# Seven block products in the second half of three output projections and of two down products

## What the reference computes

```python
x = x + (silu(gate) * sparse_attention(rms_norm(x))) @ a_w_out          # layer a
x = x + (silu(gate) * block_attention(rms_norm(x))) @ b_w_out           # layer b
proj = rms_norm_2(x) @ w_in                                             # layer c
q, k, v = split(silu(causal_conv_4(proj[dn_qkv])))                      # gated deltanet branch
q, k = l2norm(q), l2norm(k)                                             # sums of squares over a head
mixed = g_nsa * (o_nsa @ w_up_nsa) + g_dn * (o_dn @ w_up_dn)
x = x + mixed @ w_o
h2 = rms_norm_2(x)                                                      # layer d
x = x + (silu(h2 @ w_gate) * (h2 @ w_up)) @ w_down                      # 5632 hidden columns
return rms_norm_2(x)
```

## Time and profile before

| | |
|---|---|
| median of 3 runs | 2228.33 us (2227.85 to 2229.3) |
| profiled execution, its own time | 2230.15 us |
| its span, first to last instruction | 2228.8 us |
| mean granted TensorE clock | 0.999 |
| PE busy | 2208.3 us, 11376 instructions |
| DVE busy | 1529.6 us, 2034 instructions |
| ACT busy | 1216.5 us, 1682 instructions |
| POOL busy | 115.6 us |

### The profile page before, as it was taken

The page is one execution under the profiler, slowest core; times in us unless marked ns, Lnnn a source line. Parts: engine busy times, 40 slices in busy tenths (PEclk is TensorE's granted clock), DMA queues, the critical chain, the costliest instruction groups (busy, mean ns, idle before and its releaser), DMA issues.

```text
span 2228.8 us, 29092 instructions
## 1 busy us (share of the span) xinstructions
PE 2208.3 (99%) x11376; PEld 1825.2 (82%) x11376; DVE 1529.6 (69%) x2034; ACT 1216.5 (55%) x1682; POOL 115.6 (5%) x101
## 2 busy tenths in 40 slices
PE   9999999999999999999999999999999999999998
PEld 7888888888888887888888888888888888888886
DVE  5687765767765677675755556768887578855885
ACT  5545665645665664464544546556555355543554
POOL 0002210003220121000000000000000000000000
PEclk9999999999999999999999999999999999999999
DMA  7456677655677675444644446776666665665674
GB/s 257 143 176 177 196 195 232 202 189 173 201 212 233 195 209 143 142 133 147 223 161 151 151 151 196 231 213 190 210 234 200 203 197 187 214 229 177 202 243 150
DMA packets 313386, 427.31 MB, mean 192 GB/s; under 512 B 121057, under 2 KB 121217, under 8 KB 313121
## 3 DMA queue, kind: packets, MB, share of 16 engines
q1 hardware_dynamic: 311088, 418.35, 59.3%
q0 software_dynamic: 1584, 6.16, 1.0%
q10 hardware_dynamic: 576, 0.95, 0.1%
HBM read 396.06 MB, written 2.10 MB: 179 GB/s over the span
## 4 chain that ended last, share of the span: by engine, by line
PE 92%; issue 3%; DVE 2%; ACT 1%; DMA 1%; POOL 1%; SPq 0%; DVEq 0%; ACTq 0%; POOLq 0%
PE ACC L1127 19%; PE ACC L1129 19%; PE ACC L1128 19%; PE ACC L988 3%; PE ACC L989 3%; PE ACC L990 3%; PE SCPV L988 3%; PE SCPV L989 3%; PE SCPV L990 3%; PE SCPV L1060 1%; PE ACC L1059 1%; PE SCPV L1058 1%; PE SCPV L1059 1%; PE ACC L1060 1%; PE ACC L1058 1%
## 5 line engine op out<-in xcount | busy, mean ns | idle before, releaser
L2257 DVE TENSOR_TENSOR WL<-W,WH 128x1024 fp32r<-128x1024 f32 x729 | 894.0, 1234 | 399.3 <-ACT WH L1156 165.8
L1156 ACT ACTIVATE WH<-W 128x1024 fp32r<-128x1024 f32 x729 | 744.8, 1049 | 248.7 <-PE ACC L1129 93.6
L1127 PE MATMUL ACC<-WH,XH 128*128 128x512 f32 x1888 | 764.9, 405 | 4.0 <-ACT arena L1156 3.0
L1129 PE MATMUL ACC<-WH,XL 128*128 128x512 f32 x1888 | 737.1, 390 | 0.0
L1128 PE MATMUL ACC<-WL,XH 128*128 128x512 f32 x1888 | 735.4, 389 | 0.0
L1127 PEld LDWEIGHTS ACC<-WH,XH 128*128 128x128 f32 x1888 | 354.8, 188 | 80.9 <-issue 6.0
L1129 PEld LDWEIGHTS ACC<-WH,XL 128*128 128x128 f32 x1888 | 354.3, 188 | 76.5
L1128 PEld LDWEIGHTS ACC<-WL,XH 128*128 128x128 f32 x1888 | 355.2, 188 | 68.9 <-issue 1.2
L1156 ACT ACTIVATE arena<-arena 128x1024 uint16<-128x1024 uint16 (+5 forms) x98 | 87.1, 893 | 68.9 <-DVE arena L1948 26.0
L1156 ACT ACTIVATE arena<-ACC,reciprocal_roots 128x512 f32<-128x512 f32 x86 | 58.6, 687 | 118.5 <-PE ACC L1129 118.0
L988 PE MATMUL ACC<-WH,XH 128*128 128x512 f32 x264 | 103.2, 391 | 0.0
(11 more groups left out here) (378 smaller groups left out, 2657.5 us busy)
## 6 DMA issues: line engine op xcount, KB each, us to landing
W<-in_w_in SPq DMA_DIRECT2D x84, 1024.0 KB, 5.0
W<-in_a_w_in SPq DMA_DIRECT2D x47, 1024.0 KB, 5.4
W<-in_w_ffn_gate SPq DMA_DIRECT2D x44, 1024.0 KB, 5.4
W<-in_w_ffn_up SPq DMA_DIRECT2D x44, 1024.0 KB, 5.2
W<-in_w_ffn_down SPq DMA_DIRECT2D x44, 1024.0 KB, 5.2
W<-in_b_w_in SPq DMA_DIRECT2D x40, 1024.0 KB, 5.2
W<-in_a_w_out SPq DMA_DIRECT2D x16, 1024.0 KB, 5.8
W<-in_b_w_out SPq DMA_DIRECT2D x16, 1024.0 KB, 6.2
```

The lines of the kernel that those rows point to most:

```text
L1127: MM(out, hx, WH[:, k, 0:ch.width], start=q == 0 and k == 0, stop=False)
L1129: ins = MM(out, lx, WH[:, k, 0:ch.width], start=False, stop=last and k == QK - 1)
L1156: return nc.scalar.activation(out, in_, func, **how)
L2257: TT(tiles_of(M.WL[K.pair(n)], ch, half), raw, tiles_of(M.WH[n % 3], ch, half).bitcast(F32), ALU.subtract).then_inc(*did("weights_rest", n ...
```

## The change

The double chunk and the block become general. `WITH_BLOCK` names five double chunks whose third slab in order (`order_of`: slabs 0, 2, 1, 3) is a block with seven products: a.o23, b.o23, c.o23, d.p0c23 and d.p1c23. Each output projection becomes two double chunks, o01 without a block and o23 with one. b.k and b.v become b.kv, c.q0 and c.k0 become c.qk0 (c.nar follows both). d.p2c2 and d.p2c3 stay single. The block's first part is at quads 4 and 5 of the chunk; two plain quads follow.

A new block does on DVE what a pair's does (four `combine`, three `combination_rest`) and, in place of the pair's joins, eight operations of 128x512 (`joins`); ACT copies product 1 and rounds three combinations. `forms` is made for each new set of tokens (five times more; for parts 1 and 2 of the pairs again as well, since the room is shared: eight times in all), seven quads ahead of a down or projection block. The side tasks move with the chunks: `x` is now complete for two column groups at a time.

The core of the diff; the seven products themselves are the function `pair` had them in, now `seven_products`, in the same order:

```diff
+TWO = {"b.kv": ("b.k", "b.v"), "c.qk0": ("c.q0", "c.k0")}
+WITH_BLOCK = ("a.o23", "b.o23", "c.o23", "d.p0c23", "d.p1c23")
...
+def order_of(ch):
+
+    return (0, 2, 1, 3) if ch.name in WITH_BLOCK else tuple(range(ch.quads // 2))
+
+
+def place_of(ch):
+
+    return 3 if ch.taker == "pair" else 2 if ch.name in WITH_BLOCK else None
...
+            add("b.kv", one(w, 2048), "two", quads=8, fresh=x)
...
-        for c in range(NC_D):
-            add(f"{l}.o{c}", one(o, c * CH), "dve", fresh="go." + l if c == 0 else None)
+        add(f"{l}.o01", one(o, 0), "both", quads=8, fresh="go." + l)
+        add(f"{l}.o23", one(o, 2 * CH), "both", quads=8)
...
+                add("c.qk0", one(w, DN_COL), "two", quads=8, fresh="x.c")
...
+        if p < len(FF_PARTS) - 1:
+            add(f"d.p{p}c23", one("w_ffn_down_2", 2 * CH), "both", quads=2 * n, row0=done * CH, xs="H")
...
     for before, l in (("a", "b"), ("b", "c"), ("c", "d")):
-        for c in range(NC_D):
-            begin(after(f"{before}.o{c}"), "squares", l, c)
-        for c in range(3):
-            begin(after(f"{before}.o{c}") + 1, "halves", "x." + l, c)
-            begin(first(before + ".o3") + 4 * (c + 1), "joined", "x." + l, c)
-        begin(after(before + ".o3"), "halves", "x." + l, 3)
-        begin(after(before + ".o3") + 1, "roots", l)
-        begin(after(before + ".o3") + 7, "joined", "x." + l, 3)
+        for n in (before + ".o01", before + ".o23"):
+            for c in range(2):
+                begin(after(n) - 4 + 5 * c, "squares", l, int(n[-2]) + c)
+                begin(after(n) - 4 + 8 * c, "halves", "x." + l, int(n[-2]) + c)
+        for c, visit in enumerate((first(before + ".o23") + 9, first(before + ".o23") + 25, after(before + ".o23") + 3, after(before + ".o23") + 11)):
+            begin(visit, "joined", "x." + l, c)
+        begin(after(before + ".o23") + 2, "roots", l)
...
-            begin(after(f"c.{n}0") + 9 + 4 * s, "dn_conv", 0, s, c)
+            begin(after(f"c.{n}0") + 9 + 6 * (n == "k") + 4 * s, "dn_conv", 0, s, c)
             begin(after("c.v1") + 5 + 4 * (2 * c + s), "dn_conv", 1, s, c)
     for s in range(2):
-        begin(after("c.k0") + 13 + 4 * s, "dn_norms", 0, s)
+        begin(after("c.k0") + 19 + 4 * s, "dn_norms", 0, s)
...
+    def joins(b, steps):
+
+        block, to = K.blocks[b], M.JOIN[K.blocks[b].tokens]
+        g, u, col = block.quad, block.quad + 1, block.chunk.parts[0][1]
+        x = lambda t, c: M.X[:, t, col + c * CH:col + (c + 1) * CH]
+        first, second = to[:, 0, :], to[:, 1, :]
+        for i in steps:
+            if i == 0:
+                dve.wait_ge(*at("product_copied", b))
+                ins = TT(x(0, 0), first, x(0, 0), ALU.add)
+            if i == 1:
+                dve.wait_ge(*at("multiplied", g, 0, 1))
+                dve.wait_ge(*at("join_step", b, 0))
+                ins = TT(first, TP[1][:, :], first, ALU.add)
+            if i == 2:
+                dve.wait_ge(*at("multiplied", u, 0, 1))
+                dve.wait_ge(*at("join_step", b, 1))
+                ins = TT(second, PV[1][:, :], first, ALU.add)
+            if i == 3:
+                dve.wait_ge(*at("join_step", b, 2))
+                ins = TT(x(0, 1), second, x(0, 1), ALU.add)
+            if i == 4:
+                ins = TT(x(1, 1), second, x(1, 1), ALU.add)
+            if i == 5:
+                dve.wait_ge(*at("multiplied", u, 1, 1))
+                ins = TT(first, TP[0][:, :], first, ALU.add)
+            if i == 6:
+                dve.wait_ge(*at("join_step", b, 4))
+                ins = TT(x(1, 1), TP[0][:, :], x(1, 1), ALU.add)
+            if i == 7:
+                dve.wait_ge(*at("join_step", b, 5))
+                ins = TT(x(1, 0), first, x(1, 0), ALU.add)
+            ins.then_inc(*did("join_step", b, i))
...
+        if where == (-1, 0, 0):
+            combine(b, 1)
+            combine(b, 2)
+        if where == (-1, 0, 1):
+            combine(b, 3)
+        if where == (0, 0, 0):
+            combine(b, 4)
+            combination_rest(b, 2)
+        if where == (0, 0, 1):
+            if j is not None:
+                gate_left(j)
+            combination_rest(b, 4)
+            combination_rest(b, 3)
+        if where == (0, 1, 0):
+            if j is not None:
+                joined_products(j)
+            else:
+                joins(b, (0, 1, 2))
+        if where == (1, 0, 0):
+            if j is not None:
+                up_left(j)
+            else:
+                joins(b, (3, 4))
+        if where == (1, 1, 0):
+            if j is not None:
+                last_product(j)
+            else:
+                joins(b, (5, 6))
+        if where == (2, 0, 0) and j is None:
+            joins(b, (7,))
...
+        first_of = {block.tokens: b for b, block in reversed(list(enumerate(K.blocks)))}
+        ahead = lambda block: 2 if block.tokens == "gate and up 0" else 4 if block.chunk.taker == "pair" else 7
+        K.forms_at = {K.blocks[b].quad - ahead(K.blocks[b]): b for b in first_of.values()}
```

More of the change, by code:

```diff
@@ L150, with block_plan @@
 Chunk = namedtuple("Chunk", "name first quads parts width row0 k0 xs fresh taker tiles")
+def order_of(ch):
+    return (0, 2, 1, 3) if ch.name in WITH_BLOCK else tuple(range(ch.quads // 2))
+def place_of(ch):
+    return 3 if ch.taker == "pair" else 2 if ch.name in WITH_BLOCK else None
+Block = namedtuple("Block", "quad chunk tokens source slice room")
+def block_plan(chunks):
+    blocks, part = [], 0
+    for ch in chunks:
+        if ch.taker != "pair" and ch.name not in WITH_BLOCK:
+            continue
+        if ch.taker == "pair":
+            part = sum(int(ch.name[4:]) >= start for start in FF_STARTS) - 1
+            tokens, source, room = f"gate and up {part}", "x.d", "d"
+        elif ch.xs == "H":
+            tokens, source, room = f"down {part}", f"h{part}.d", "d"
+        else:
+            tokens, source, room = ch.name[0], {"a": "go.a", "b": "go.b", "c": "mx.c"}[ch.name[0]], ch.name[0]
+        place = place_of(ch)
+        blocks.append(Block(ch.first + 2 * place, ch, tokens, source, order_of(ch)[place], room))
+    return blocks
 def weight_plan():
@@ L194, in weight_plan @@
         add(f"c.ud{c}", one("w_up_dn_2", c * CH), "dve", quads=2, k0=8, fresh="od.c" if c == 0 else None)
-    for c in range(NC_D):
-        add(f"c.o{c}", one("w_o_2", c * CH), "dve", fresh="mx.c" if c == 0 else None)
+    add("c.o01", one("w_o_2", 0), "both", quads=8, fresh="mx.c")
+    add("c.o23", one("w_o_2", 2 * CH), "both", quads=8)
     done = 0
@@ L996, in pair, with seven_products @@
+    def seven_products(ch, x, visit, ends):
+        b, hi, lo = K.block_at[ch.first + 2 * place_of(ch)], M.hi[ch.xs], M.lo[ch.xs]
+        block = K.blocks[b]
+        g, u = block.quad, block.quad + 1
+        tokens = lambda a, t, k: a[:, QK * x + k:QK * x + k + HK, t * P:(t + 1) * P]
         A11, A12, A22 = [(tokens(hi, t, k), tokens(lo, t, k)) for t, k in ((0, 0), (0, HK), (1, HK))]
-        S1, S2, S3, S4 = [(M.form_hi[:, i], M.form_lo[:, i]) for i in range(4)]
-        place = lambda n, half: (M.WH[n % 3][:, half * HK:(half + 1) * HK, :], M.WL[K.pair(n)][:, half * HK:(half + 1) * HK, :])
@@ L1000, in product @@
[L1000 removed]
+        form_hi, form_lo = M.FORMS[block.room]
+        S1, S2, S3, S4 = [(form_hi[:, i], form_lo[:, i]) for i in range(4)]
+        weights = lambda n, half: (M.WH[n % 3][:, half * HK:(half + 1) * HK, :], M.WL[K.pair(n)][:, half * HK:(half + 1) * HK, :])
+        def product(out, form, w, first, last):
             nonlocal visit
             for k in range(HK):
[L1003 to L1005 removed]
+                MM(out, form[0][:, k, :], w[0][:, k, :], start=first and k == 0, stop=False)
+                MM(out, form[0][:, k, :], w[1][:, k, :], start=False, stop=False)
+                ins = MM(out, form[1][:, k, :], w[0][:, k, :], start=False, stop=last and k == HK - 1)
@@ L1010, in pair @@
             for half in range(2):
-                pe.wait_ge(*at("turned", ch.fresh, 6 + half))
+                pe.wait_ge(*at("turned", ch.fresh, 2 * x + half))
         pe.wait_ge(*at("weights_rest", g, 0))
-        if j:
-            pe.wait_ge(*at("product_copied", j - 1))
-        product(PV[0][:, :], A11, place(g, 0), first=True, last=True).then_inc(*did("product", j, 1))
+        wait_empty("PV0")
+        product(PV[0][:, :], A11, weights(g, 0), True, True).then_inc(*did("product", b, 1))
@@ L1532, in narrow, with take @@
         yield
-    def take(ch, t):
-        l, name = ch.name[0], ch.name[2:]
+    def take(ch, t, second=None):
+        l, name, banks, last = ch.name[0], ch.name[2:], M.ACC, ch.first + ch.quads - 1
+        if second is not None:
+            name, banks, last = TWO[ch.name][second][2:], (M.ACC, SC)[second], ch.first + ch.quads - 2 + second
         if ch.tiles != QK:
@@ L1541, in take @@
             return
[L1542 removed]
+        acc = banks[t][:, 0:ch.width]
         s = scale_of(l, t)
```

401 lines of the change are left out of this document (211 added, 190 removed).

## The result

The changed kernel takes 2237.63 us (median of 5, 2236.17 to 2239.37); the kernel before, with these runs, 2228.99 (2227.85 to 2229.48). The ratio is 1.0038, 95% interval 1.0027 to 1.0050: slower by some 8.6 us, where the forecast was 2231.0 and its range ended at 2235.0. The profiled execution has a span of 2238.1 us, 9.3 over that of before.

The account below looks back on a forecast made before the run. The prediction took the kernel to be bound by PE's number of matmuls; -7.1 + 0 + 4.8 + 5.2 = +2.9 us on 2228.33 gave, rounded, 2231.0 us, range 2224.0 to 2235.0.

Parts of the forecast that it names:

- What is taken away, 6.8 us: On PE, five blocks save one product each, 30 matmuls at 0.2274 us: 6.8 us, 7.1 with 0.3 for fewer bank waits.
- The five blocks at nothing: In the five new blocks, DVE's added work costs nothing, covered by 0.7 us of slack; bounds 0 to 3.5 in all.
- The seams, 4.8 us: At a to b, b to c, c to d, PE waits for a rest behind join and roots: 1.6 us each, 4.8.
- the 0.65 us of the next rest: At each seam, the next half quad's rest, behind four XL operations and a copy, comes 0.65 us late.
- The start of layer c, 5.2 us: A load behind two transposes comes 5.5 us late; PE's norm sums wait 5.2 us for k0's squares; bounds 1.5 to 5.5.
- wrong if the norm sums wait under 1 us: Test for layer c's start, where the norm-sum matmuls were to wait some 5 us for an activation.
- the sum: Over the whole kernel, -7.1 + 0 + 4.8 + 5.2 = +2.9 us.
- a pitch of 0.2274 kept: Sign in the changed kernel's profile: PE's matmuls keep starting 0.2274 us apart.
- (C): Each new block waits as d.gu0's did, 3.2 us atop both stalls: 2234.3; chance 0.23 with page's rule and upper bounds.
- (A): All stalls at the seams and layer c's start are hidden: 2221.2 us; chance 0.15.
- (B): Only one place stalls: 2226.4 us with the c stage alone, 2226.0 with the seams alone; chance 0.20.
- rule on table loads: Table loads in layer c and seams also drain, 2.66 us per switch, some 11 us more; chance 0.02.

Follow-up runs that it names:

- second: Changed kernel with roots one visit earlier and column group 2's turning four visits later at the three seams: 2232.16 us, ratio 1.0013 to the kernel before.
- fifth experiments: Changed kernel with roots earlier, group 2's turning later, k0's raw tile four visits later, its convolutions and norm sums two visits later: 2230.95 us, ratio 1.0008.
- the filled run: Changed kernel with thrown-away matmuls put before c.q1's first and second visit (20, 10) and d.gu0's third product (20): 2233.31 us, ratio 1.0019.

## Why the prediction was wrong, point by point

- **What is taken away, 6.8 us.** Right. It shows where nothing else was changed on the path: 2.3 us where 2.7 were due with two blocks, 4.4 where 4.1 were due with three, each to some 2 us.
- **The five blocks at nothing.** Right for the five: no wait of a block's matmul but d.gu0's. Wrong in that only the new blocks were costed. The old block of d.gu0 stands four to six quads behind the seam, and its forms and rests begin as soon as DVE is done with the last column group, which is now later: 2.26 us where there were 0.57. I had even used d.gu0 as a rival for the new blocks, and had not asked what the change does to d.gu0 itself.
- **The seams, 4.8 us.** The mechanism was right, and the second and fifth experiments show it: 5.5 us, and 0.6 with the order changed. The term was under-sized at c to d, where the transpose took 5.7 us to land, not 4.3 (2.5 us of wait, not 1.6), and over-sized at a to b (0.9). The prediction had laid out the XL behind the same transpose as well, as the 0.65 us of the next rest; what it did not see is that with the roots moved ahead this wait alone is 1.8 us, so that mending the first gives nothing.
- **The start of layer c, 5.2 us.** The lateness of the load was right within 0.3 us. The place was wrong: the step "what feels it is the squares of k0" passed over the takes of c.v0's banks, which stand ahead of the last silus in the same list. The waits there are 3.3 us (2.27 and 1.07) and not 5.2. By its own test ("wrong if the norm sums wait under 1 us") this point failed.
- **The step that failed is the sum.** It had a term for each wait and none for what a wait does to the matmuls behind it; "a pitch of 0.2274 kept" stood among the signs without a reason. The clock costs 2.6 us at c.q1 and 1.6 at d.gu0 in the trace, and the filled run gives back 4.3 of the 8.6 us that the changed kernel lost. With this term and d.gu0's 1.7 us the forecast of +2.9 would have been +8.8. That it would so nearly meet the measured 8.6 is in part luck: the term for layer c was too large by 2.4 us (5.2 against the 2.3 of the larger L1175 line and the 0.5 of the small tables), and 1.9 us are not itemised.
- **The rivals.** (C) had a time (2234.3) nearer than the forecast, for a reason that did not occur: no new block waits. (A) and (B) are refuted, as both places stall.

The Trainium skill's rule on table loads that the prediction weighed (page "ScalarE: Activation LUTs", "What ACT_TABLE_LOAD costs") was not seen here either: in the changed kernel's trace a load starts at 810.32, takes 1.28 us, and the next activation starts at 811.62, with no drain between.

## What to carry to other kernels

When PE is busy for 99% of the span, a wait that the change adds is to be priced twice: its length, and the stretch behind it at half the clock. Here the two stretches cost 4.2 us behind 5.6 us of waits; two other waits of 1.6 and 1.7 us in the same execution cost no more than their length, and where the next wait is for DVE, a slow stretch is in part paid back there. And a change that shortens PE's work also brings the next stage's needs nearer: before believing the saving, walk through every in-order queue at the next seam and ask what stands behind the latest transfer, to the end of the list, not to the first wait found; then ask the same of the next tight place behind it. Three of the five blocks, where no such list is near, give 4.4 us; all five give none.

## What the runs showed of the hardware that was not expected

The clock's answer to a wait is not the same each time. In the profiled executions a wait of 1.6 us at the start of layer c (757.96) or of 1.7 at that of d (1533.99) was followed by no slow stretch in the changed kernel, one of 2.26 at d.gu0 by eight matmuls at 0.427 us; in the run with the seams mended the two waits before c.q1 (2.25 us the longer) left the clock at 1.00, and the one of 2.43 at d.gu0 brought it to 0.57:

```profile
816.00:824.00 8.00, 5.06 (x22) 3.55 (x20) 7.86 (x20) 6.29 (x10) 0.00 (x0) 1.00 0.48 159
824.00:830.00 6.00, 5.53 (x32) 4.90 (x33) 5.89 (x10) 3.36 (x5) 2.09 (x2) 1.00 0.68 181
1549.00:1555.00 6.00, 3.57 (x16) 2.65 (x15) 5.97 (x6) 4.38 (x5) 0.00 (x0) 1.00 0.01 3
1555.00:1559.00 4.00, 4.00 (x12) 3.13 (x11) 4.00 (x5) 2.69 (x3) 0.00 (x0) 0.57 0.50 128
```

It also changes from one execution of a kernel to the next: without blocks, the executions with a mean clock of 0.999 took 2233.5 and 2234.0 us, the one with 0.998 2234.4, those with 0.997 2236.1 to 2238.8. So such waits widen a kernel's spread (5 us there, 2 with three blocks), and one profile can miss what they cost. With the roots one visit earlier the clock fell behind a wait of 1.78 us at the seam a to b and not behind the longer ones of 2.26 before c.q1 and 2.23 at d.gu0, so the length of a wait alone doesn't decide it. What does stays open.
